# A decoder layer on eight cores: second-tile norm transposes and tile-1 pooling moved behind projection matmuls

## What is computed

```python
def layer(x, pool_hist, conv_hist, start_pos, mk, mv, ...):
    h = rmsnorm(x, g_mix)
    u = h @ w_in
    a = u[..., :POOL_WIDTH]
    val = u[..., POOL_WIDTH:POOL_WIDTH + CONV_CH]
    gate = u[..., POOL_WIDTH + CONV_CH:]
    glu = val * jax.nn.sigmoid(gate)
    a_ext = jnp.concatenate([pool_hist, a], axis=1)
    g_ext = jnp.concatenate([conv_hist, glu], axis=1)
    ya = pool_mixer(a_ext, start_pos, pool_map_w, pool_map_b, pool_scale)
    yb = conv_mixer(g_ext, conv_dw_w, conv_dw_b, conv_ln_g, conv_ln_b)
    x = x + jnp.concatenate([ya, yb], axis=-1) @ w_out
    x = x + cross_attn(rmsnorm(x, g_attn), mk, mv, w_q, w_o)
    h = rmsnorm(x, g_ffn)
    x = x + (jax.nn.silu(h @ w_gate) * (h @ w_up)) @ w_down
```

## Time and profile before

| | us |
|---|---|
| two timed runs | 1230.56 and 1283.52, median 1257.04 |
| profiled execution | 1213.74 |
| its span, slowest core (core 7) | 1212.2 |
| spans of the eight cores | 1161.7 to 1212.2 |
| PE busy on core 7 | 1070.6 |
| DVE busy, ACT busy | 571.2, 437.2 |

### The profile page before, as it was taken

The page is one execution under the profiler, slowest core; times in us unless marked ns, Lnnn a source line. Parts: engine busy times, 40 slices in busy tenths (PEclk is TensorE's granted clock), DMA queues, the critical chain, the costliest instruction groups (busy, mean ns, idle before and its releaser), DMA issues.

```text
span 1212.2 us, 18373 instructions; the slowest of 8 cores (1161.7 to 1212.2 us)
## 1 busy us (share of the span) xinstructions
PE 1070.6 (88%) x5904; PEld 539.5 (45%) x5904; DVE 571.2 (47%) x1083; ACT 437.2 (36%) x816; POOL 69.0 (6%) x92
## 2 busy tenths in 40 slices
PE   1787997859989999999992699988998999999993
PEld 1345864325444444444441348744444444444441
DVE  4464347311555554656345765463244244254347
ACT  6323367244743232323126521773554101101115
POOL 1000000001201010110100000001000000000000
PEclk9998998968998888899996699998887889999997
DMA  9505028352987979694266204044930072453203
GB/s 241 96 1 88 16 35 122 54 106 73 156 125 122 151 106 152 98 137 60 42 90 205 74 0 72 1 70 64 165 53 1 1 105 38 67 79 39 41 1 141
DMA packets 62094, 99.63 MB, mean 82 GB/s; under 512 B 2760, under 2 KB 33608, under 8 KB 61973
## 3 DMA queue, kind: packets, MB, share of 16 engines
q0 software_dynamic: 54608, 74.65, 42.7%
q1 hardware_dynamic: 7397, 23.82, 6.0%
HBM read 162.40 MB, written 12.12 MB: 144 GB/s over the span
## 4 chain that ended last, share of the span: by engine, by line
PE 79%; DMA 6%; ACT 6%; DVE 6%; issue 3%; POOL 0%; DVEq 0%; ACTq 0%; SPq 0%; POOLq 0%
PE ps L273 76%; DMA arena<-w_in 4%; DMA y<-arena 2%; ACT arena L380 2%; DVE arena L491 2%; ACT arena L393 2%; PE ps L1131 1%; PE ps L407 1%; DVE arena L430 1%; ACT L382 1%; DVE arena L667 1%; ACT arena L382 1%; DVE arena L828 1%; DVE arena L1104 0%; DVE arena L826 0%
## 5 line engine op out<-in xcount | busy, mean ns | idle before, releaser
L273 PE MATMUL ps<-arena 128*128 128x512 bf16 (+2 forms) x5304 | 1011.6, 352 | 23.8 <-ACT arena L830 10.7
L273 PEld LDWEIGHTS ps<-arena 128*128 128x128 bf16 x5304 | 491.3, 101 | 527.2 <-issue 238.1
L430 DVE TENSOR_TENSOR arena<-arena,ps 128x512 f32<-128x512 f32 (+1 forms) x272 | 183.1, 685 | 80.4 <-PE ps L273 70.1
L1346 DVE TENSOR_TENSOR arena<-ps,arena 128x512 bf16<-128x512 f32 (+1 forms) x110 | 63.7, 587 | 238.6 <-PE ps L273 178.1
L1344 ACT ACTIVATE arena<-ps 128x512 f32<-128x512 f32 (+1 forms) x110 | 55.3, 514 | 264.6 <-PE ps L273 261.6
L407 PE MATMUL ps<-arena 128*128 128x128 bf16 (+1 forms) x424 | 40.7, 255 | 88.2 <-ACT arena L393 85.9
L380 ACT ACTIVATE arena<-arena 128x1024 bf16<-128x1024 f32 (+1 forms) x70 | 73.5, 1050 | 62.5 <-DVE arena L430 61.2
L412 DVE TENSOR_TENSOR arena<-ps,arena 128x1024 bf16<-128x1024 bf16 (+1 forms) x53 | 61.0, 1166 | 44.5 <-PE ps L407 44.4
L407 PEld LDWEIGHTS ps<-arena 128*128 128x128 bf16 (+1 forms) x424 | 32.4, 116 | 102.0 <-issue 99.4
L393 ACT ACTIVATE arena<-arena 128x1024 bf16<-128x1024 f32 (+1 forms) x53 | 59.5, 1134 | 1.3 <-issue 1.0
L1104 DVE SCALAR_TENSOR_TENSOR arena<-arena,ps 128x256 f32<-128x256 bf16 x128 | 53.9, 421 | 12.7 <-DVE arena L1104 0.9
(11 more groups left out here) (95 smaller groups left out, 406.9 us busy)
## 6 DMA issues: line engine op xcount, KB each, us to landing
arena<-x SPq DMA_DIRECT2D x16, 512.0 KB, 6.4
arena<-ck POOLq DMA_DIRECT2D x16, 512.0 KB, 10.2
arena<-cv POOLq DMA_DIRECT2D x16, 512.0 KB, 7.8
arena<-w_gate POOLq DMA_DIRECT2D x8, 1024.0 KB, 14.2
arena<-w_up POOLq DMA_DIRECT2D x8, 1024.0 KB, 19.3
arena<-w_down POOLq DMA_DIRECT2D x8, 1024.0 KB, 17.7
y<-arena SPq DMA_DIRECT2D x16, 512.0 KB, 2.9
arena<-w_in POOLq DMA_DIRECT2D x6, 1024.0 KB, 25.4
```

Source lines behind the costliest of these rows:

```text
L273: ins = e.matmul(out=out_ap, lhsT=l, rhs=r, start=(i == 0), stop=(i == n - 1))
L430: dve(lambda e, xs_=xs_, pv=pv: e.tensor_tensor(out=xs_, in0=xs_, in1=pv, op=ALU.add), [bs, s_X[u]], [s_X[u]])
L1346: dve(lambda e, bu=bu, i=i, j=j, c0=c0, n=n: e.tensor_tensor(out=intv[:, j, c0:c0 + n], in0=psf(bu)[:, 0:n], in1=fsgv[:, i, 0:n], op=ALU.m ...
```

## The change

The nine units of pass 0 are no longer all transposed ahead of the projections. Units 0 to 3 go through their whole norm; units 4 to 7 only through ACT's part, and their transposes and evictions (`late_B`) come behind tile 0's projections, ahead of tile 0's pooling. The norm of the sample unit 8 is written ahead of TS's projections. In pass 0 the pooling of tile 1 is kept in a list and written behind TS's projections. The four diagonal builds come after all of ACT's work. The `hs` buffers get a ring counter of their own, and `PreNorm` holds up to two scaled units back in place of one.

```diff
--- before.py
+++ after.py
@@ -362,7 +362,7 @@
                   writes=[s])
             return v, s
 
-        hs_ring = {"i": 0}
+        hs_ring = {"i": 0, "h": 0}
         s_stat = [AR.slot("st") for _ in range(8)]
         AR.alloc("sqj", D * 2)
         s_sqj = AR.slot("sqj")
@@ -372,9 +372,9 @@
         s_ots = AR.slot("ots")
 
         def stats_rstd(xin, s_in, rows):
-            i = hs_ring["i"] % 4
             j_ = hs_ring["i"] % 8
             hs_ring["i"] += 1
+            i = j_
             st = stv[0:rows, 4 * j_:4 * j_ + 4]
             s_st = s_stat[j_]
             act(lambda e: e.activation(out=sqjv[0:rows, :], in_=xin, func=AF.Square, accum_out=st[:, 0:1]),
@@ -388,7 +388,9 @@
             return (xin, s_in, rows) + stats_rstd(xin, s_in, rows)
 
         def norm_A2(a1, hsv, s_hs):
-            xin, s_in, rows, i, st, s_st = a1
+            xin, s_in, rows, _, st, s_st = a1
+            i = hs_ring["h"] % 4
+            hs_ring["h"] += 1
             hs = hsv[0:rows, i, :]
             act(lambda e: e.activation(out=hs, in_=xin, func=AF.Copy, scale=st[:, 2:3]),
                 [s_in, s_st], [s_hs[i]])
@@ -552,30 +554,42 @@
               gtv = AR.view("gt", BF16, "p (c t) -> p c t", c=4)
               s_gt = [[AR.slot("gt") for _ in range(3)] for _ in range(4)]
 
-              pa, pb = [], []
               pre_done = prefetch.pop("norm1", None)
+              late_B = []
               if pre_done is not None:
                   pre_done()
                   for c_ in range(4):
                       build_diag(c_)
-              for n_, u in enumerate([] if pre_done is not None else units):
-                  pa.append((u, norm_A1(xu(u), s_X[u], urows(u))))
-                  if len(pa) > 1:
-                      uu, a1 = pa.pop(0)
-                      pb.append((uu,) + norm_A2(a1, hsv, s_hs))
-                  if len(pb) > 1:
+              else:
+                  pa, pb = [], []
+
+                  def _b1():
                       uu, hs_, sh_ = pb.pop(0)
                       c0_, nn_ = ucols(uu)
                       norm_B(hs_, sh_, urows(uu), C_GMIX, Av[:, :, c0_:c0_ + nn_], [s_A[f][uu] for f in range(8)])
-                  if 2 <= n_ < 6:
-                      build_diag(n_ - 2)
-              while pa:
-                  uu, a1 = pa.pop(0)
-                  pb.append((uu,) + norm_A2(a1, hsv, s_hs))
-              while pb:
-                  uu, hs_, sh_ = pb.pop(0)
-                  c0_, nn_ = ucols(uu)
-                  norm_B(hs_, sh_, urows(uu), C_GMIX, Av[:, :, c0_:c0_ + nn_], [s_A[f][uu] for f in range(8)])
+
+                  for n_, u in enumerate(T0[1]):
+                      pa.append((u, norm_A1(xu(u), s_X[u], urows(u))))
+                      if len(pa) > 1:
+                          uu, a1 = pa.pop(0)
+                          pb.append((uu,) + norm_A2(a1, hsv, s_hs))
+                      if len(pb) > 1:
+                          _b1()
+                  while pa:
+                      uu, a1 = pa.pop(0)
+                      pb.append((uu,) + norm_A2(a1, hsv, s_hs))
+                  while pb:
+                      _b1()
+                  for u in T1[1]:
+                      pa.append((u, norm_A1(xu(u), s_X[u], urows(u))))
+                      if len(pa) > 1:
+                          uu, a1 = pa.pop(0)
+                          late_B.append((uu,) + norm_A2(a1, hsv, s_hs))
+                  while pa:
+                      uu, a1 = pa.pop(0)
+                      late_B.append((uu,) + norm_A2(a1, hsv, s_hs))
+                  for c_ in range(4):
+                      build_diag(c_)
 
               dve(lambda e: e.tensor_copy(out=gtv[:, :, 0:30], in_=gthv[:, :, 0:30]), [s_gth],
                   [s_gt[c][0] for c in range(4)])
@@ -602,9 +616,12 @@
                   s_gl = [AR.slot("gl") for _ in range(4)]
 
               sgi = [0]
+              deferred_pool = []
               for t_i, us in tiles:
                   c0, n = tcols(us)
                   is_s = us[0] == 8
+                  if is_s:
+                      norm_unit(8, C_GMIX, Av, s_A, hsv, s_hs)
                   rd_A = lambda: [s_A[f][u] for f in range(8) for u in us]
                   ai = t_i % 2
                   for j in range(4):
@@ -642,7 +659,16 @@
                           dve(lambda e, bv=bv, si=si, j=j, g0=g0: e.tensor_tensor(
                               out=gtv[:, j, g0:g0 + 512], in0=psf(bv)[:, 0:512], in1=sgv[:, si, 0:512], op=ALU.mult),
                               [bsv, s_sg[si]], [s_gt[j][1 + t_i]])
-                  if not is_s:
+                  if t_i == 0:
+                      for (uu, hs_, sh_) in late_B:
+                          c0_, nn_ = ucols(uu)
+                          norm_B(hs_, sh_, urows(uu), C_GMIX, Av[:, :, c0_:c0_ + nn_], [s_A[f][uu] for f in range(8)])
+                  if is_s:
+                      for fn_ in deferred_pool:
+                          fn_()
+                      deferred_pool = []
+
+                  def pooling(t_i=t_i, us=us, c0=c0, ai=ai):
                       first_global = (ps_i == 0 and t_i == 0)
                       if t_i == 0:
                           dve(lambda e, ai=ai: e.tensor_copy(out=atv[:, ai, :, 0:15], in_=athv[:, :, 0:15]),
@@ -697,6 +723,14 @@
                           out_toks.append(P.dma("sp", lambda e: e.dma_start(out=pp_d, in_=ppov[0:15, :]), reads=[s_ppo]))
                           AR.free("ppo")
 
+                  if not is_s:
+                      if t_i == 0 or not has_s:
+                          pooling()
+                      else:
+                          deferred_pool.append(pooling)
+              for fn_ in deferred_pool:
+                  fn_()
+
               AR.free("sg")
               AR.free("pt")
               AR.free("hs")
@@ -1303,7 +1337,7 @@
                       self.pa.append((u, norm_A1(xu(u), s_X[u], urows(u))))
                       if len(self.pa) > 1:
                           self._a2()
-                      if len(self.pb) > 1:
+                      if len(self.pb) > 2:
                           self._b()
 
                   def _a2(self):
```

## The result

The changed kernel takes 1249.95 us (median of 11 runs, 1235.58 to 1287.22), the kernel before on the same chip 1232.4 (10 runs, 1209.62 to 1283.52). The ratio is 1.028 with an interval of 1.015 to 1.042, where "within 2%" and 4.8 us more had been forecast: slower, though 2% lies inside the interval.

A forecast was written before the change was run, and what follows sets the result against it. PE on the slowest core was taken as the bound, its work before 49.77 us covered by the w_in load. 6.2 + 1.7 - 3.1 + 0 = +4.8 us, added to 1222.1, forecast 1227 us, range 1207 to 1264.

The forecast's parts named there:

- part 1: Before the first projections: transposing only four units up front gains 0, since the w_in load covers PE until 49.77 us.
- Part 2: Between tiles 0 and 1: four late transposed units and their evictions delay tile 1 by 6.2 us, plus 1.7 for slow restart.
- The restart: Tile 1's matmuls behind PE's 3.8 us idle gap run at a lower clock: +1.7 us, bounds 0 to 2.
- rival C: Dense stretches behind PE's added idle gaps get 0.02 less mean clock: 24.3 us slower, 1238 us profiled; chance 0.08.
- Part 3: Behind tile 1: the sample unit's late norm, projection and added table load let L713 start 9.9 us after tile 1.
- Part 4: Tile 1's pooling behind the sample's products removes L713's 13.0 us delay, 9.9 replaces it: -3.1 us; later pooling stays covered.
- Part 5: Between the passes: the hs ring and longer prefetched-norm lag change 0, bounds -1.1 to +1; y's one buffer sets the path.
- The +4.8: Whole kernel on core 7: 6.2 + 1.7 - 3.1 + 0 us slower, 1218.5 us against the profiled execution.
- +8: Upper bound of the slowdown: core 0's restart adds 1.7 us and the sample's matmuls at half clock 1.7.
- A: Pass 0: L713's stall goes whole and late transposes are hidden, 9.7 us faster, 1204 us profiled; chance 0.12.
- B: Between the passes: PE's 17.5 us wait is on the path and is won, 1201 us profiled; chance 0.04.
- D: Pass 0: the w_in wait or removed stall covers what is added; no effect, within 2 us of 1214; chance 0.14.

The follow-up runs named there:

- late_only: Kernel before with only units 4 to 7 transposed behind tile 0's projections, diagonal builds late; 1183.23 us in its only execution, no ratio.
- defer_ec_loads: Kernel before with tile 1's pooling behind the sample's products, ec at the arena's top, SP's gfin and state loads held until w_in landed; 1157.45 us, ratio 0.9868.
- spread_ec: Changed kernel with ec at the arena's top and the four late transposed units spread over tile 0's val and gate groups; 1176.32 us, ratio 0.9984 to before.
- the four repeats: Changed kernel unedited, timed again against the kernel before; ratios 1.0117, 1.0140 and 1.0133, one run too scattered for a ratio.
- after_ec: Changed kernel with only buffer ec moved to the arena's top, over memory tile 1's pooling doesn't use; 1180.09 us, ratio 1.0052 to before.
- defer_ec: Kernel before with tile 1's pooling moved behind the sample's products and ec at the arena's top; 1163.29 us, ratio 0.9904.
- defer_only: Kernel before with only tile 1's pooling moved behind the sample's products, ec left in place; 1177.35 us, ratio 1.0007.
- lag_only: Kernel before with only the separate hs ring counter and the prefetched norm holding two units back; 1178.52 us, ratio 1.0002.

## Why the prediction was right or wrong

**The path and the cover (what bounds the kernel, part 1): right.** The gate group starts at 49.7 to 50.8 on all cores, as before, and `late_only` gained nothing ahead of it. That what is hidden there is hidden by one load was right too: with the load faster (`defer_ec_loads`) the wait goes.

**Part 2, 6.2 for the transposes: right.** 6.5 us from the end of tile 0 to the start of tile 1 (64.53 to 71.06), 4.58 of it idle. The profile names L674 as its releaser, a copy that starts right behind the four evictions which tile 1 reads:

```profile
66.21 4.61 DVE L414 TENSOR_TENSOR arena<-ps,arena 128x1024 bf16<-128x1024 bf16 x4
```

The restart, put at +1.7, was right as well, its upper bound of 2 a little short. Sixteen matmuls without a gap take 3.46 us (55.33 to 58.79 in `spread_ec`), so 96 take 20.8; tile 1 took 22.57 on cores 6 and 7 and 22.3 to 23.3 on all cores of the four repeats, 1.5 to 2.5 more. On cores 0 to 5 of the first profile it took 25.2 to 27.6. That is not the restart: core 1 is back at 0.98 from 75 to 80 as core 7 is, and falls to 0.81 only after it (the rows above). It belongs to rival C.

`late_only` has both terms by themselves: 9.1 us for 6.2 + 1.7, in one execution.

**Part 3, 9.9 for the sample unit: right.** Tile 1 ends at 93.6 and L747 starts at 103.56, 9.9 behind it. The table loads cost their 1.28 us, and the work behind them starts at once:

```profile
95.54 1.28 ACT L382 ACT_TABLE_LOAD   x1
96.83 0.29 ACT L382 ACTIVATE arena<-arena 16x1 f32<-16x1 f32 x1
```

The second added load, for the sigmoid, has no gap behind it either (it ends at 102.94, L647 starts at 102.96). The further 2.8 us, which the prediction estimated from the Trainium skill (ScalarE: Activation LUTs, What ACT_TABLE_LOAD costs), are not there.

**Part 4: the step that failed.** "Where does the pooling go?" was asked only of what reads the pooling's results: the pool maps and the load of w_out. Both came out as said: neither waits. It was not asked of what writes into memory that the pooling uses. ACT's first copy into `ec` does, and the price is a wait of 7.6 us and a cold convolution (17.43 for 15.5), 9.5 us together. With `ec` moved, `after_ec` has neither: its yardstick, which ends where the convolution starts, is 9.0 shorter, its time 8.3. `defer_ec` against `defer_only` shows much the same on the kernel before (yardstick 44.8 and 53.1, and again both convolution times). So part 4 was worth -3.1 as worked out, plus 9.5 that it didn't have.

**Part 5: right.** `lag_only` is 1.0002.

**Sum.** The +4.8 is close to what `after_ec` measures, 5.4 us on the yardstick and 6.1 in time. With the buffer it is 14 to 16, a mean of 1.3%, above the +8 that was the mechanism's bound, but still "within 2%" at the clocks of the better chips. The first comparison has 20 us more on its slowest cores, and they lie with the clock. **Rivals.** A fell: the transposes are not hidden where the change puts them; `spread_ec` shows where they are. B fell by `lag_only`. D fell: 14.2 us on core 7. C, held at 0.08, was right on the side and on what set the size on the slowest cores: their dense stretches were granted 0.81, and the mean of the slowest core is 0.018 lower (0.881 for 0.899), where C took 0.02. The prediction set it aside because a restart lasts only microseconds. It had core 7's mean of 0.899 before it and did not ask where that comes from; it is not restarts but long stretches at 0.81, as the row of 400 to 500 us shows. That the added idle stretches cause the low clock is not shown.

## What to carry to other kernels

When work is moved later on an engine, ask of it not only who reads what it writes, but who writes what it reads: with buffers that reuse freed memory every later allocation over it is a waiter, though no data goes between them. Before a wait is taken away, follow the next instruction on each engine that it had held back, and price what it meets. Work that stands between two dense stretches belongs in small pieces inside the first, so that its hand-over lies beside matmuls.

## What the runs showed of the hardware

An idle stretch of 4.6 us on PE cost 1.5 to 2.5 us more in the 96 matmuls behind it (22.3 to 23.3 us in place of 20.8, all cores of the four repeats); one of 7.6 us cost the convolution's first 132 matmuls 1.9 (17.43 for 15.5) and 2.2 in `defer_only`. A second kind of slowness is longer: in some executions pairs of cores were granted 0.81 in dense stretches, as cores 0 to 5 from 80 us on in the first profile of the changed kernel, and core 7 from 400 to 500 in the kernel before. A load in the background is not free: with 1.9 MB less beside it the last third of w_in landed 36.0 us after its issue in place of 45.7. And the same kernel's steady difference of 1.2 to 1.4% on three chips read 2.8% on one where nearly all pairs of cores had a mean clock below 0.93.
